# Attention stage: the last keys scored one tile earlier, copies of turned probabilities on one engine, weight chunks split earlier

## The reference, cut to what matters

```python
h = concatenate([meta, x])                 # 16 + 512 rows, 1024 columns
hn = rms_norm(h, attn_norm)
q, k, v, g, f = split(hn @ fox_w_in)       # 16 heads of 64
q, k = rms_norm(q), rms_norm(k)            # per head
c = cumsum(log_sigmoid(f + b_f))           # decay of each head
s = q @ k.T / 8 + c[query] - c[key]        # causal
o = softmax(s) @ v * sigmoid(g)
h = h + o @ fox_w_out
```

## Time and profile before

| | us |
|---|---|
| median of 3 runs (lowest, highest) | 1674.96 (1672.22, 1680.48) |
| the profiled execution, its own time | 1673.88 |
| its span, first to last instruction | 1672.1 |
| PE, DVE, ACT, POOL busy in the span | 1459.7, 423.4, 474.3, 601.4 |
| mean granted TensorE clock | 0.955 of 2.4 GHz |

### The profile page before, as it was taken

How to read it: one execution, slowest core, us unless ns; L and a number is a source line. 1 busy time by engine, 2 the same in 40 slices (tenths; PEclk the granted TensorE clock), 3 DMA queues, 4 the chain that set the end, 5 groups by cost and what they waited for, 6 DMA issues and landing times.

```text
span 1672.1 us, 21702 instructions
## 1 busy us (share of the span) xinstructions
PE 1459.7 (87%) x8130; PEld 987.0 (59%) x8130; DVE 423.4 (25%) x1089; ACT 474.3 (28%) x1042; POOL 601.4 (36%) x710
## 2 busy tenths in 40 slices
PE   6999988878999999997988998949998888888881
PEld 5688865556888888886676435724444444444440
DVE  3003057623111101112154122261221111111114
ACT  3326356533222222223353012211221111111111
POOL 3344544334444444443354013322332222222222
PEclk9999999889999999999999998969999999999996
DMA  3332311012222233321212007358999999999974
GB/s 121 107 120 79 112 31 36 27 54 98 85 87 83 99 101 101 101 76 61 105 56 96 1 1 258 136 232 318 396 397 405 404 402 396 392 389 391 387 283 156
DMA packets 91461, 300.14 MB, mean 179 GB/s; under 512 B 12980, under 2 KB 35664, under 8 KB 66816
## 3 DMA queue, kind: packets, MB, share of 16 engines
q1 hardware_dynamic: 83136, 283.37, 45.0%
q0 software_dynamic: 8160, 15.75, 2.6%
q10 hardware_dynamic: 96, 0.08, 0.0%
HBM read 294.94 MB, written 12.62 MB: 184 GB/s over the span
## 4 chain that ended last, share of the span: by engine, by line
PE 64%; DMA 19%; DVE 8%; SPq 3%; ACT 2%; issue 2%; POOL 2%; ACTq 0%; POOLq 0%; DVEq 0%
PE ps L1001 14%; PE ps L1002 13%; PE ps L1003 13%; DMA big<-in_moe_w_dram 8%; DMA wring<-in_moe_w_dram 7%; PE ps L1413 5%; PE ps L1362 4%; SPq L626 3%; PE ps L1439 3%; DMA hT<-in_moe_w_dram 2%; PE ps L1158 1%; PE ps L1400 1%; DVE wring L1604 1%; PE ps L1187 1%; PE ps L1170 1%
## 5 line engine op out<-in xcount | busy, mean ns | idle before, releaser
L464 POOL TENSOR_TENSOR wring_halves<-wring,wring_halves 128x512 fp32r<-128x512 f32 x262 | 338.4, 1295 | 385.1 <-ACT wring_halves L459 384.4
L459 ACT CAST wring_halves<-wring 128x512 fp32r<-128x512 f32 x262 | 159.6, 619 | 438.3 <-PE ps L1003 415.4
L1001 PE MATMUL ps<-wring_halves,big_halves 128*128 128x512 f32 x560 | 224.3, 401 | 27.1 <-POOL wring_halves L464 23.6
L1001 PE MATMUL ps<-hT_halves,wring_halves 128*128 128x512 f32 (+1 forms) x496 | 194.9, 393 | 6.5 <-DVE big_halves L1506 5.3
L1002 PE MATMUL ps<-big_halves,wring_halves 128*128 128x512 f32 (+1 forms) x496 | 194.4, 392 | 0.0
L1003 PE MATMUL ps<-hT_halves,wring_halves 128*128 128x512 f32 (+1 forms) x496 | 194.4, 392 | 0.0
L2156 POOL DMA_INDIRECT y_dram<-xn,sidx x64 | 57.0, 891 | 325.8 <-DVE xn L1918 318.5
L1002 PE MATMUL ps<-wring_halves,hT_halves 128*128 128x512 f32 x384 | 153.8, 401 | 0.0
L1003 PE MATMUL ps<-wring_halves,hT_halves 128*128 128x512 f32 x384 | 153.5, 400 | 0.0
L1413 PE MATMUL ps<-big,arena 128*32 128x256 f32 x1024 | 124.4, 394 | 29.8 <-DMA big<-in_moe_w_dram 29.2
L1001 PEld LDWEIGHTS ps<-wring_halves,big_halves 128*128 128x128 f32 x560 | 107.8, 193 | 54.2 <-POOL wring_halves L464 27.7
(11 more groups left out here) (322 smaller groups left out, 1939.3 us busy)
## 6 DMA issues: line engine op xcount, KB each, us to landing
big<-in_moe_w_dram SPq DMA_DIRECT2D x86, 1024.0 KB, 23.9
wring<-in_moe_w_dram SPq DMA_DIRECT2D x66, 1024.0 KB, 26.0
wring<-in_ffn_w_in_dram SPq DMA_DIRECT2D x22, 1024.0 KB, 6.6
hT<-in_moe_w_dram SPq DMA_DIRECT2D x20, 1024.0 KB, 22.9
wring<-in_fox_w_in_dram SPq DMA_DIRECT2D x7, 2048.0 KB, 8.1
wring<-in_gla_w_in_dram SPq DMA_DIRECT2D x6, 2048.0 KB, 8.0
mkv<-in_moe_w_dram SPq DMA_DIRECT2D x10, 1024.0 KB, 30.2
xn<-in_moe_w_dram SPq DMA_DIRECT2D x10, 1024.0 KB, 30.2
```

The source lines that it names most:

```text
L459: act.copy(hi, src).then_inc(s_hi, 1)
L464: pool.tensor_tensor(lo, src, hi, ALU.subtract).then_inc(s_lo, 1)
L1001: pe.matmul(out, lhs[1], rhs[0], start=start, stop=False)
```

## The change

- **Scores.** The last 16 keys of tile i = 3 are scored right behind tile i = 2, into free columns (400 to 415) of tile 2's banks. `scores(s+2)` stands ahead of `pv(s-1)` in every step. `rowmax` takes the 16 columns as its first cut, and the next pair's first scores wait for that (`s_sp`). The wait for `qk_out` goes from `scores` to `ptrans` of tile 3.
- **Copies.** `pt_out` is on ACT for both heads of all tiles; DVE has none.
- **Output chunks.** The halves of wo0's first three chunks go to free places of the arena, on ACT behind `pt_out` of the last pair's tiles 0, 1 and 2, and on POOL ahead of `out_low(7)`.
- **Meta rows.** For k1, v0 and v1, `meta_rows` comes after the tile's second chunk; the units are renumbered.
- **Exp.** ACT takes one small Exp before it waits for the first transposed keys.
- **Start.** DVE asks for the next tile's root before it scales the one before, and makes the meta rows' halves after the tiles' low halves; `forget_by_head` waits for them (`s_hm`).

```diff
-        arena, hTm2 = with_halves("arena", 6144, 3328, 2 * KD * META)
+        arena, arenar = with_halves("arena", 6144, 0, 6144)
+        hTm2 = arenar[:, 3328:3328 + 2 * KD * META]
...
+        early_halves = [(arenar[:, a:a + 512], arenar[:, b:b + 512]) for a, b in ((0, 512), (1152, 2176), (3712, 4224))]
...
+        META_EARLY = (("k", 1), ("v", 0), ("v", 1))
...
+                if (name, j) in META_EARLY:
+                    unitsB.append((name, j, T, "A"))
                 unitsB += [(name, j, t, "A" if name == "g" else "AD"[t % 2]) for t in range(T)]
                 ends = (s_mB, len(unitsB))
-                if name in "kv":
+                if (name, j) == ("k", 0):
                     unitsB.append((name, j, T, "A"))
...
+            if 0 <= c - attn_end < len(early_halves):
+                return (src,) + early_halves[c - attn_end]
...
             if c == attn_end:
+                act.wait_ge(s_qkt, 2 * PAIRS + 1)
+                act.wait_ge(s_S, NS - T)
+                act.wait_ge(s_mx, 2 * (NS - T))
+            if c == attn_end + len(early_halves):
                 act.wait_ge(s_pv, NS)
                 act.wait_ge(s_mx, 2 * NS)
...
             if a >= 512:
-                return bank(QB)[:, e * META + a - 512:e * META + b - 512]
+                return bank((s % 2) * 2 + e)[:, a - 112:b - 112]
...
             act.wait_ge(s_small, 16 * 3)
+            act.activation(rsum[:, 0:1], rsq[:, 0:1], ACT.Exp).then_inc(s_exp, 1)
+            act.wait_ge(s_exp, 1)
             act.wait_ge(s_qkt, 1)
...
             def pt_out(s):
                 i = s % T
-                for e in range(1 + second_by_act(s)):
+                for e in range(2):
                     act.wait_ge(s_T, 2 * s + e + 1)
                     if e == 0 and s >= 2:
                         act.wait_ge(s_pv, s - 1)
                     if i < T - 1:
                         act.copy(PTm[s % 2][e], ptmbank(i, e))
-                    last = act.copy(PT[s % 2][e][:, 0:P * (i + 1)], ptbank(e)[:, 0:P * (i + 1)])
-                    if i == T - 1:
-                        act.wait_ge(s_T, 2 * s + 2)
+                    elif e:
                         o = 3712 + 2 * CB + (s % 2) * 2 * P
-                        last = act.copy(arena[0:META, o:o + 2 * P], bank(QB)[0:META, P:3 * P])
-                    last.then_inc(s_ptA, 1)
+                        act.copy(arena[0:META, o:o + 2 * P], bank(QB)[0:META, P:3 * P])
+                    act.copy(PT[s % 2][e][:, 0:P * (i + 1)], ptbank(e)[:, 0:P * (i + 1)]).then_inc(s_ptA, 1)
...
+                if p == PAIRS - 1 and i < len(early_halves):
+                    high_half(act, attn_end + i)
...
+                    if k == 1 and (name, j) in META_EARLY and not n:
+                        meta_rows(name, j)
...
             def forget_by_head():
...
+                pe.wait_ge(s_hm, 1)
...
             def scores(s):
...
-                if i == T - 1:
-                    pe.wait_ge(s_qkA, min(2 * p + 5, 2 * PAIRS + 1))
-                    if p:
-                        pe.wait_ge(*probsT_out(s - T, 0))
-                        pe.wait_ge(*probsT_out(s - T, 1))
...
+                if i == 0 and p:
+                    pe.wait_ge(s_sp, p)
+                todo = [(s, 0, min(n, 512))] + ([(s + 1, 512, L)] if i == T - 2 else [])
+                for r, a, b in todo:
                     for e in range(2):
...
+                    if i == T - 1:
+                        pe.wait_ge(s_qkA, min(2 * p + 5, 2 * PAIRS + 1))
...
-                if i != 1 and s + 2 < NS:
+                if s + 2 < NS:
                     scores(s + 2)
...
+            def root_of_tile(t):
+                dve.wait_ge(s_ss, t + 2)
+                root_of(rstd[:, t:t + 1], ss[:, t:t + 1])
+
+            def scaled_tile(t):
+                dve.wait_ge(s_pw, t + 2)
+                dve.tensor_scalar(xn[:, t, :], xres[:, t, :], rstd[:, t:t + 1], None, ALU.mult).then_inc(s_xn, 1)
...
+            root_of_tile(1)
+            scaled_tile(0)
...
+            root_of_tile(2)
+            scaled_tile(1)
+            root_of_tile(3)
+            scaled_tile(2)
             dve.tensor_scalar(qgain, qgain, float(HD) ** -0.5, None, ALU.mult).then_inc(s_gain, 1)
...
+            scaled_tile(3)
+            tp_out(0, gcols[:, 0:KD])
...
-            for t in range(T):
-                normed_tile(t, t + 2)
-            tp_out(0, gcols[:, 0:KD])
...
-                cuts = [(0, n - P), (n - P, min(n, 512))] + ([(512, n)] if n > 512 else [])
+                cuts = ([(512, n)] if n > 512 else []) + [(0, n - P), (n - P, min(n, 512))]
...
-                if s:
-                    pt_out(s - 1)
                 normed_probs(s)
...
+            low_halves(attn_end, attn_end + len(early_halves))
             out_low(PAIRS - 1)
-            low_halves(attn_end, wo_end)
+            low_halves(attn_end + len(early_halves), wo_end)
```

More of the change, by code:

```diff
@@ L217, in program @@
         s_first = sem("first_weights_in")
+        s_hm = sem("meta_halves_ready")
         s_gz = sem("gain_rows_zeroed")
@@ L250, in program @@
         s_S = sem("scores_ready")
-        s_sp = sem("first_spill_done")
+        s_sp = sem("last_keys_read")
         s_mx = sem("row_max_ready")
@@ L377, in program @@
         first_of = {v[:2]: u for u, v in reversed(list(enumerate(unitsB)))}
+        unit_of = {v[:3]: u for u, v in enumerate(unitsB)}
         attn_end = len(chunks)
@@ L504, in ptmbank @@
             return bank(QB)[0:META, (1 + e) * P:(2 + e) * P] if i == T - 1 else ptbank(e)[0:META, 3 * P:4 * P]
-        def second_by_act(s):
-            return s % T < 2
         def probsT_out(s, e):
-            if e == 0 or second_by_act(s):
-                n = sum(1 + second_by_act(r) for r in range(s)) + 1 + e
-                return s_ptA, n
-            return s_ptD, sum(not second_by_act(r) for r in range(s + 1))
+            return s_ptA, 2 * s + e + 1
         block = ctx.enter_context(nc.Block())
@@ L1050, in project @@
                         forget_by_token()
-                    elif (tile, k) == ("v1", 4):
+                    if k == 1 and (name, j) in META_EARLY and not n:
+                        meta_rows(name, j)
+                    if (tile, k) == ("v1", 4):
                         meta_keys()
@@ L1056, in meta_rows @@
             def meta_rows(name, j):
-                u = first_of[name, j] + T
+                u = unit_of[name, j, T]
                 free(unitsB, u, s_eA, s_eD)
@@ L1117, in meta_keys @@
                 pe.wait_ge(s_kam, 1)
-                pe.wait_ge(s_eA, evacs(unitsB, first_of["v", 0] + T))
+                pe.wait_ge(s_eA, evacs(unitsB, unit_of["v", 0, T - 2]))
+                pe.wait_ge(s_eD, evacs(unitsB, unit_of["v", 0, T - 1]))
                 for p in range(PAIRS):
@@ L1123, in qk @@
             def qk(p, i):
-                if p == 0 and i == 0:
-                    pe.wait_ge(s_eA, evacs(unitsB, first_of["v", 0] + T))
-                    pe.wait_ge(s_eD, evacs(unitsB, first_of["v", 0] + T - 1))
                 pe.wait_ge(s_stage, 2 * p + i + 1)
@@ L1145, in scores @@
                     pe.wait_ge(s_mx, 2 * (s - 1))
-                if i == T - 1:
-                    pe.wait_ge(s_qkA, min(2 * p + 5, 2 * PAIRS + 1))
-                    if p:
-                        pe.wait_ge(*probsT_out(s - T, 0))
-                        pe.wait_ge(*probsT_out(s - T, 1))
-                for a in range(0, n, 512):
-                    b = min(n, a + 512)
-                    for e in range(2):
-                        r = slice(e * HD, (e + 1) * HD)
-                        if a and e:
-                            last.then_inc(s_sp, 1)
-                            pe.wait_ge(s_sp, p + 1)
-                        last = pe.matmul(sbank(s, e, a, b), QT[p % 2][r, i * P:(i + 1) * P], KT[p % 2][r, a:b], start=True, stop=True)
+                if i == 0 and p:
+                    pe.wait_ge(s_sp, p)
+                todo = [(s, 0, min(n, 512))] + ([(s + 1, 512, L)] if i == T - 2 else [])
+                for r, a, b in todo:
+                    for e in range(2):
+                        d = slice(e * HD, (e + 1) * HD)
+                        last = pe.matmul(sbank(r, e, a, b), QT[p % 2][d, r % T * P:(r % T + 1) * P], KT[p % 2][d, a:b], start=True, stop=True)
                 last.then_inc(s_S, 1)
@@ L1221, in _ @@
                     qk(p + 1, 1)
-                if i == 1 and s + 2 < NS:
-                    scores(s + 2)
             pv(NS - 1)
@@ L1600, in rowmax @@
                         d = P * i + a - (n - P)
-                        bias = cb[p % 2][e][:, a:b] if m == 0 or i == T - 1 else cbm[p % 2][e][:, d:d + b - a]
+                        bias = cb[p % 2][e][:, a:b] if a == 0 or i == T - 1 else cbm[p % 2][e][:, d:d + b - a]
                         last = m == len(cuts) - 1
@@ L1608, in rowmax @@
                             ins.then_inc(s_mx, 1)
+                        elif a >= 512 and e:
```

(3 more changed lines are left out.)

32 lines of the change are left out of this document (12 added, 20 removed).

## The result

| | before | changed |
|---|---|---|
| median (lowest, highest), us | 1674.26 (1672.22, 1680.48), 4 runs | 1648.78 (1647.01, 1650.78), 4 runs |
| profiled execution: own time, span | 1673.88, 1672.1 | 1647.72, 1646.0 |
| PE, DVE, ACT, POOL busy | 1459.7, 423.4, 474.3, 601.4 | 1448.4, 419.3, 482.6, 605.1 |
| mean granted clock | 0.955 | 0.959 |

A forecast was written before the change was run, and what follows sets the result against it. PE was taken to bound the kernel (busy 1459.7 of 1672.1 us), with order deciding in attention, where no engine is full. Terms 12.0 + 3.4 + 3.5 + 0.9 + 4.3 = 24.1 gave 1650 us, range 1641 to 1662.

The forecast's parts named there:

- pairs, order and copies: Attention pairs: score order and copies on ACT together gain 1.5 us a pair, 12.0 over eight pairs (2.4 to 17.6).
- clock in the pairs: Attention: 6.8 us lost to clock drops over seven steps; half, 3.4, comes back with PE's hole gone.
- output chunks (tail): Between last pv and wo0: ready chunks close PE's 4.01 us gap, less 0.5 on ACT: 3.5 (2.5 to 4.0).
- entry: Entry of attention: meta rows and early Exp bring the first exponential 0.9 us earlier (0 to 1.3).
- start: Kernel start: overlapped roots bring the last scaling and first product earlier, by 4.3 us (3.0 to 5.0).
- Scores of tile 3 first: Each attention pair: earlier scores cut DVE's wait from 2.37 to 0.3 us and remove PE's hole, 1.5 a pair.
- Copies: Attention pairs: moving DVE's copies to ACT gains nothing on balance; ACT busy 10.9, DVE 9.9 us a pair.
- The lead should come through whole: Later stages: each waits for the stage before, so time saved ahead of them reaches the end in full.
- slow restart of the output product: Output product: 2 us of slow restart, counted only in the clock term's upper bound (6.8 + 2).
- the clock stays up wholly: Rival: every drop follows a PE hole the change closes; other 3.4 and 2 us come too, 1645; chance 0.25.
- Serial copies: Rival, attention pairs: ACT's serial copies take the hole's place, pairs give 2.4, clock nothing, 1664; chance 0.12.
- A pair bound by ACT: Rival, attention: ACT becomes the bound, each pair 2.2 us longer, 8.9 slower in all, 1684; chance 0.04.

The follow-up runs named there:

- e8: Changed kernel with the fourth tile's scores back in their old order and the second head's copies of tiles 2 and 3 back on DVE: 1670.29 us, ratio 0.998.
- e1b: Changed kernel with the fourth tile's scores back in their old order and place, all copies still on ACT: 1672.54 us, ratio 0.998 to before.
- e2b: Changed kernel with the second head's copies of tiles 2 and 3 back on DVE, new score order kept: 1649.13 us, ratio 0.982 to before.
- e10: e9 with the second head's copies of tiles 2 and 3 back on DVE: 1644.51 us, ratio 0.980 to before.
- e3b: Changed kernel without the three early chunks of wo0: 1650.80 us, ratio 0.985 to before.
- e4b: Changed kernel with one more wait on POOL, so wo0's early low halves follow DVE's last normalization: 1641.19 us, ratio 0.979 to before.
- e4c: Same edit as e4b, run again beside the changed kernel on one chip: 1641.31 us, ratio 0.978 to before.
- e11: The changed kernel run again without any edit: 1648.48 us, ratio 0.982 to before.
- e7: e4b with a second POOL wait, so k0's first low halves follow DVE's last scaling: 1644.67 us, ratio 0.982 to before.
- e9: e4c with k1's meta rows back behind its token tiles, v0's and v1's still early: 1639.55 us, ratio 0.978 to before.
- e6: Changed kernel with meta rows behind all four token tiles and without the early Exp: 1650.17 us, ratio 0.985 to before.

## Why the prediction was right, and where it was off

| term | predicted | found in the profile |
|---|---|---|
| pairs, order and copies | 12.0 | 13.2 |
| clock in the pairs | 3.4 | 7.4 |
| output chunks (tail) | 3.5 | 1.7 |
| entry | 0.9 | 1.05 |
| start | 4.3 | 3.6 |
| not priced: clock at 82 to 86 | | -1.1 |
| sum | 24.1 | 25.8 |

The right column is the lead at wo0. It comes so: seven steps took 111.13 and take 92.23. Undisturbed, the old ones would be 14.71, five of 14.89, and 14.61 for the last, which has no next pair (e8's row for it), 103.8 in all; so the clock's part is 7.4 and the order's 11.5. Another 1.6 comes between the first exponential and the first fourth scores.

*Scores of tile 3 first: right.* I took 1.5 a pair from the hole on PE, with undisturbed steps of 14.90; measured is 14.89 - 13.43 = 1.46. DVE's wait was put at 0.3 and is 0.32; ACT's busy time of a pair at 10.9 and is 10.47; the new wait for `s_sp` shows nowhere. DVE is busy 10.40 where I had 9.9. What I had not priced is the last step: the missing next pair makes it 1.55 shorter than the others, and in the old order only 0.29 (14.90 and 14.61 in e8). These 1.3 are what 13.2 has over 12.0. e1b and e8 show the whole from the other side: without the order the other parts, 8.5 us by their terms (3.6, 1.05 and a tail 3.9 shorter), are measured at 0.2%, 3 us. In e8's profile they are 6.8 us at wo0 and 4.3 at the end; ahead of the attention its clock is 0.76 at 76 to 90, where the kernel before has 1.00.

*Copies: right*, and by two comparisons: e2b in the new order, e1b with e8 in the old, each at equal clocks. e10's 5 us show only that the tail is near a fall of the clock.

*The clock: the mechanism right, the size half.* "With the hole gone PE idles perhaps 0.7 of 13.4 us, and the reason for the drops with it": PE idles 1.24, but all of the loss went, as no pair falls below 1.00, and e1b brings hole and drops back together. I halved the term for fear that the new mix would make other drops. They did come, but outside the seven steps: in the last pair, at 82 to 86 and at 744 to 748. By the rule of the Trainium skill ("TensorE: Matmul & The Clock Gate", Part 4: PE-mode transpose), that transposes do not count as busy in the way matmuls do, the clock could have fallen at `ptrans` and `qk` too. In the pair above they are 7.0 us (3.3, 2.1 and 1.6, the groups with `ident`) of the 15.9 that the busy times of all six groups of products add up to (they overlap), and the clock was 1.00 over 92 us: no sign of it here.

*Output chunks: the step that failed.* "With three chunks ready PE goes on at once" is right: no gap ahead of wo0. Wrong was that the only price is ACT's 0.5. The low halves that POOL takes in the last pair fall on the normalization for which PE waits, and the clock falls behind these waits. It takes the new order and the early chunks together: in the old order (e8) the first two low halves end as that normalization begins, and the 4 us come. I had the sign of it in the start's rows, used it there, and did not ask it here. e3b against the changed kernel shows that nothing was left of the 4.0; e4b and e4c give them back by moving POOL alone. The 1.7 by which the tail shrank is owed to the order and the clock with it: e3b has it without early chunks, at a clock of 1.00 up to the last `pv`, where the kernel before had 0.73 over its last pair.

*Entry: right* (1.05 for 0.9). The table load took 1.28 us there and 1.28 here, at 208.22 in ACT's idle time.

*Start: the mechanism right, 0.7 too much (1.9 by e11's profile).* The last scaling began at 12.59 (I had 12.4) and took 1.72. I added half a microsecond for the case that POOL does not slow it; e7 shows that even then nothing comes of it, since the 32 transposes of PE, 5.13 us from 10.66, end behind it. I had not set PE's own work against the chain through DVE.

*The lead should come through whole: nearly.* 25.8 at wo0, 26.1 at the end, between 24.9 and 27.7 on the way. The 2 us for the slow restart of the output product were gained (27.7). They went again: 1.1 up to the end of the SwiGLU layer, which I cannot place, and 1.7 behind it. There PE stalls for POOL 2.3 us in both kernels, and in this profile only in the changed one the clock falls behind it: first its row of the timeline and its stretch, then those of the kernel before:

```profile
743.53 0.47 PE L1008 MATMUL ps<-wring_halves,big_halves 128*128 128x512 f32 x1 [2.31 <-POOL wring_halves L476]
```

```profile
744.00:746.00 2.00, 2.00 (x6) 1.57 (x6) 0.00 (x0) 0.00 (x0) 0.00 (x0) 0.52 0.71 188
```

```profile
770.15 0.47 PE L1001 MATMUL ps<-wring_halves,big_halves 128*128 128x512 f32 x1 [2.33 <-POOL wring_halves L464]
```

```profile
770.00:772.00 2.00, 1.85 (x8) 1.60 (x9) 0.00 (x0) 0.00 (x0) 0.00 (x0) 1.00 0.47 90
```

That fall is not tied to the kernel: in e11 PE stalls for POOL the same 2.31 us, up to 744.37, and the clock stays at 1.00. By e11's profile the lead is 22.3 at wo0 and 25.7 at the end. So the gain at the end is sure, and that a lead is handed on unchanged is not.

*The total.* That the forecast was off by only 1.2 us is in part luck. In the table the clock and the pairs gave 5.2 more than priced, and the output chunks, the start and the fall at 82 to 86 took back 3.6.

Of the rivals, "the clock stays up wholly" described the seven steps but not the last pair; its ground, that every drop follows a hole which the change closes, does not hold, as in the kernel before the clock also falls behind PE's stall at 396.31 (0.50 at 398 to 400). e4c, where the last pair keeps its clock too, is at 1641.31, below the 1645 that this rival gave. Serial copies show as the 0.8 us a pair for which PE waits for ACT, within the 1 us that was allowed, and a step is only 0.07 shorter without them (e2b). A pair bound by ACT left no trace.

## What to carry to other kernels

Where PE waits once in each round of a loop for a result of its own earlier work, issue that work first, and look at the stretches for the clock: here the hole was 1.4 us a pair, and what the clock lost behind it another 1.05 us (7.4 over seven steps). Before filling an idle engine with early work, look for what it shares with the engine on the path: POOL's idle time in the last pair was free, DVE's pace beside it was not, and one more wait on POOL was worth 7 us of the median, 3.6 of them in its own stage. Compare stretches only at equal clocks, else a fall of the clock is read as the price of an edit, and do not price an edit by one profile.

## What the runs showed of the hardware

- DVE's normalization of 400 columns, two instructions, took 0.77 us with POOL idle, 1.23 in a full pair and 2.83 beside POOL's subtraction of float32 halves; the scaling of 1024 columns 0.75 and 1.72; the normalization of 528 columns 0.90 and, in e8, 1.48. POOL's two subtractions took 2.50 alone and 2.62 to 2.95 beside DVE: the slower engine hardly pays.
- The clock fell without any idle time in the record: at 82 in the changed kernel and in e9, PE busy 2.00 of 2 us in each stretch, behind 4.1 us of 16-column products. Twelve of the fourteen profiles have such a fall between 78 and 90; the kernel before and e6 had the same products and no fall.
- The same 32 transposes at the start took 5.13 us in the changed kernel's profile and 6.60 in e11's, with a granted clock of 1.00 in the rows of both.
- The same wait can end in either clock (e9 and e10 at 320; and in one kernel, 2.31 us before 743.53 in the changed kernel's profile with 0.52 behind it, 2.31 us before 744.37 in e11's with 1.00), while the pairs' 1.4 us hole was followed by a fall in four of seven steps before, in four in e8 and in seven in e1b.
